# GpSimd sums half of the shift pieces of three quarters, and five small moves around them

## What is computed

```python
c_act = jax.nn.silu(c)
mod = c_act @ w_ada[l] + b_ada[l]                 # 2048 x 6144, one row
shift, scale, gate = jnp.split(mod, 3, axis=-1)
h = rms_norm(x, norm_g[l]) * (1 + scale[:, None]) + shift[:, None]
proj = h @ w_in[l]                                # 256 x 2048 times 2048 x 13824
pool_u, pool_z, q, k, v, attn_z, conv_a, conv_b, conv_z, gates = jnp.split(proj, split_idx, axis=-1)
# three branches (trailing-window pooling, windowed attention, gated causal convolution),
# each times silu of its z, projected, times its sigmoid gate, summed to merged
x = x + gate[:, None] * (merged @ w_out[l])
return rms_norm(x, final_g)
```

## Time and profile before

| | us |
|---|---|
| median of 3 runs | 956.42 (956.16 to 956.43) |
| the profiled execution | 956.62 |
| its span in the trace | 954.8 |
| TensorE busy in the span | 914.2 (96%) |
| VectorE busy | 686.2 (72%) |
| ScalarE busy | 417.4 (44%) |
| GpSimd busy | 10.0 (1%) |

### The profile page before, as it was taken

The page is one execution under the profiler, slowest core; times in us unless marked ns, Lnnn a source line. Parts: engine busy times, 40 slices in busy tenths (PEclk is TensorE's granted clock), DMA queues, the critical chain, the costliest instruction groups (busy, mean ns, idle before and its releaser), DMA issues.

```text
span 954.8 us, 10317 instructions
## 1 busy us (share of the span) xinstructions
PE 914.2 (96%) x4243; PEld 740.6 (78%) x4243; DVE 686.2 (72%) x793; ACT 417.4 (44%) x375; POOL 10.0 (1%) x27
## 2 busy tenths in 40 slices
PE   1799999989999999999999999999999999999996
PEld 1467686878888888888888888888888888887884
DVE  4767696768968867767778776595677878756663
ACT  3436152634344343443474655447433333434332
POOL 2000000000000000000000000000000000000000
PEclk9899999999999999999999999999999999999998
DMA  9999999855446565665544444554779998955512
GB/s 327 382 387 387 360 366 352 301 161 172 140 154 220 178 206 189 189 208 176 177 158 155 140 166 137 174 178 171 243 247 393 375 329 304 323 188 198 176 45 88
DMA packets 107790, 220.01 MB, mean 230 GB/s; under 512 B 3696, under 2 KB 3776, under 8 KB 106976
## 3 DMA queue, kind: packets, MB, share of 16 engines
q1 hardware_dynamic: 106336, 212.88, 64.7%
q0 software_dynamic: 1120, 5.43, 1.5%
q10 hardware_dynamic: 288, 1.05, 0.3%
HBM read 217.25 MB, written 2.10 MB: 230 GB/s over the span
## 4 chain that ended last, share of the span: by engine, by line
PE 88%; DMA 5%; DVE 3%; ACT 2%; issue 1%; SPq 0%; DVEq 0%; ACTq 0%
PE acc_odd L1107 13%; PE acc_odd L1109 13%; PE acc_even L1107 13%; PE acc_odd L1108 13%; PE acc_even L1109 12%; PE acc_even L1108 12%; DMA raw<-in_w_in 4%; PE side_a L1107 1%; ACT wh L429 1%; PE side_a L1109 1%; PE side_a L1108 1%; DVE wl L679 1%; DMA x_tok<-in_x 1%; PE side_b L1278 1%; DVE ada_sums L716 1%
## 5 line engine op out<-in xcount | busy, mean ns | idle before, releaser
L679 DVE TENSOR_TENSOR wl<-raw,wh 128x2048 fp32r<-128x2048 f32 x151 | 345.4, 2290 | 195.5 <-ACT wh L429 195.0
L429 ACT ACTIVATE wh<-raw 128x2048 fp32r<-128x2048 f32 x151 | 288.3, 1913 | 290.1 <-PE acc_even L1109 114.5
L1107 PE MATMUL acc_even<-wh,act_h 128*128 128x512 f32 x432 | 172.5, 399 | 6.0 <-DVE wl L727 3.2
L1107 PE MATMUL acc_odd<-wh,act_h 128*128 128x512 f32 x432 | 170.0, 394 | 0.7 <-DVE part_u L772 0.7
L1109 PE MATMUL acc_even<-wh,act_l 128*128 128x512 f32 x432 | 169.3, 392 | 0.0
L1108 PE MATMUL acc_even<-wl,act_h 128*128 128x512 f32 x432 | 169.2, 392 | 0.0
L1109 PE MATMUL acc_odd<-wh,act_l 128*128 128x512 f32 x432 | 168.3, 390 | 0.0
L1108 PE MATMUL acc_odd<-wl,act_h 128*128 128x512 f32 x432 | 168.1, 389 | 0.0
L1107 PEld LDWEIGHTS acc_even<-wh,act_h 128*128 128x128 f32 x432 | 81.8, 189 | 25.6 <-issue 4.6
L847 DVE SCALAR_TENSOR_TENSOR conv_slots<-conv_slots,taps 128x256 f32<-128x256 f32 x240 | 100.2, 479 | 0.2
L1107 PEld LDWEIGHTS acc_odd<-wh,act_h 128*128 128x128 f32 x432 | 81.1, 188 | 18.3 <-DVE part_u L772 1.1
(11 more groups left out here) (270 smaller groups left out, 892.6 us busy)
## 6 DMA issues: line engine op xcount, KB each, us to landing
raw<-in_w_in SPq DMA_DIRECT2D x107, 1024.0 KB, 5.1
raw<-in_w_ada SPq DMA_DIRECT2D x48, 1024.0 KB, 9.1
raw<-in_w_out SPq DMA_DIRECT2D x16, 1024.0 KB, 5.0
raw<-in_w_branch_pool SPq DMA_DIRECT2D x8, 1024.0 KB, 5.0
raw<-in_w_branch_attn SPq DMA_DIRECT2D x8, 1024.0 KB, 5.0
raw<-in_w_branch_conv SPq DMA_DIRECT2D x8, 1024.0 KB, 6.0
raw<-in_conv_pw SPq DMA_DIRECT2D x4, 1024.0 KB, 5.1
x_tok<-in_x SPq DMA_DIRECT2D x2, 1024.0 KB, 8.9
```

What stands on the lines that cost most here:

```text
L429: nc.scalar.activation(wh[:, m % RING], raw[SLOT_OF[g]][:, :, :], ACT.Copy).then_inc(high_done, 1)
L679: nc.vector.tensor_tensor(wl[:, m % RING], raw[SLOT_OF[load_of(m)]][:, :, :], wh[:, m % RING].bitcast(F32), ALU.subtract).then_inc(raw_don ...
L1107: nc.tensor.matmul(sums, xh, wh[:, slot, i, :], start=begin, stop=False)
```

## The change

Six edits. First, of the four shift pieces of each of the quarters 1 to 3, pieces 0 and 1 are no longer multiplied by TensorE: GpSimd multiplies each of their row tiles with its column of c (in place), and adds them up in `gate_sums`, a buffer that is unused at that time: 7 instructions for piece 0 and 8 for piece 1, each waiting for the one before. The slot is free when GpSimd is done. TensorE reduces that sum over partitions with four one-column matmuls behind the scale sums, and VectorE adds the four columns to the shift. Pieces 2 and 3 stay at j = 3 and 4. Second, `pool_w` is loaded behind all this and behind the last `h_ready`. Third, the low half of the very first piece is made tile by tile, so that TensorE may start on tile 0. Fourth, from `glu_a` on, VectorE takes each last part one step earlier. Fifth, so it does with the low halves of `merged` near the end (steps 131 to 137 in place of 132 to 138). Sixth, the last scaling is shared 1280 : 768 columns between VectorE and ScalarE in place of 1024 : 1024, and the stores with it.

```diff
+def by_pool(load):
+    return load[0] == "shift" and load[1] > 0 and load[2] < 2
...
-    HALF = D_MODEL // 2
+    SHARE = 1280
...
-                if before >= 0 and LOADS[before][0] == "shift":
-                    sp.wait_ge(shift_done, shifts(before))
+                if before >= 0 and by_pool(LOADS[before]):
+                    sp.wait_ge(pool_summed, pool_shifts(before))
+                elif before >= 0 and LOADS[before][0] == "shift":
+                    sp.wait_ge(shift_done, pe_shifts(before))
...
-            pool.wait_ge(x_t, 4)
+            pool.wait_ge(consts_ready, 1)
+            pool.wait_ge(c_ready, 1)
+            for q in range(1, QUARTERS):
+                if q > 1:
+                    pool.wait_ge(mod_t, q)
+                for i in range(2):
+                    g = LOAD_OF["shift", q, i]
+                    pool.wait_ge(loaded[SLOT_OF[g]], landed(g))
+                    for t in range(PK):
+                        src, column = raw[SLOT_OF[g]][:, t, :], c_act[:, PK * i + t:PK * i + t + 1]
+                        dst = src if i or t else gate_sums[:, :]
+                        last = nc.gpsimd.tensor_tensor(dst, src, column.broadcast_to([P, COLS]), ALU.mult)
+                        if i or t:
+                            chained(last)
+                            last = nc.gpsimd.tensor_tensor(gate_sums[:, :], gate_sums[:, :], src, ALU.add)
+                        if t < PK - 1:
+                            chained(last)
+                    last.then_inc(pool_summed, 1)
+                    pool.wait_ge(pool_summed, 2 * q - 1 + i)
+            pool.wait_ge(h_ready, KT)
             pool.dma_start(pool_w[:, :, :, :], a["pool_w"][0].rearrange("g (k p) n -> p g k n", p=P)
                            ).then_inc(pool_w_loaded, 16)
-            pool.wait_ge(h_ready, KT)
...
+            def first_split_tile(t):
+                dve.wait_ge(first_high, 1)
+                nc.vector.tensor_tensor(wl[:, 0, t, :], raw[SLOT_OF[load_of(0)]][:, t, :], wh[:, 0, t, :].bitcast(F32),
+                                        ALU.subtract).then_inc(first_low, 1)
...
+                if q:
+                    chained(nc.vector.tensor_tensor(mod_shift, mod_shift, pb[:, 1 + PK:1 + 2 * PK], ALU.add))
...
             hidden_tile(0)
-            first_split(0)
+            first_split_tile(0)
             hidden_tile(1)
-            first_split(1)
+            first_split_tile(1)
+            first_split_rest()
...
-                if m == 23:
+                if m == 22:
                     dve.wait_ge(*freed("b0"))
...
-                if m in (24, 25, 26, 27, 28):
-                    last_part(OPEN[m - 22])
+                if m in (23, 24, 25, 26, 27):
+                    last_part(OPEN[m - 21])
...
-                if m in (132, 134, 136, 138):
-                    j = (m - 132) // 2
+                if m in (131, 133, 135, 137):
+                    j = (m - 131) // 2
...
-                half = x_res[:, h, 0:HALF]
+                half = x_res[:, h, 0:SHARE]
...
-                if q and i == 0:
+                first = 2 if q else 0
+                if q and i == first:
                     pe.wait_ge(mod_ready, q)
...
                 if q:
-                    ins = scale_sums(q)
+                    scale_sums(q)
+                    pe.wait_ge(pool_summed, pool_shifts(LOAD_OF["shift", q, 3]))
+                    for t in range(PK):
+                        ins = nc.tensor.matmul(pb[:, 1 + PK + t:2 + PK + t], gate_sums[:, P * t:P * (t + 1)], ones[:, 0:1],
+                                               start=True, stop=True)
...
-                    if 1 <= j < 5:
+                    if 3 <= j < 5:
                         shift_piece(k + 1, j - 1)
```

More of the change, by code:

```diff
@@ L95, in shifts, with pool_shifts, pe_shifts @@
     return sum(load[0] == "shift" for load in LOADS[:g + 1])
+def by_pool(load):
+    return load[0] == "shift" and load[1] > 0 and load[2] < 2
+def pool_shifts(g):
+    return sum(by_pool(load) for load in LOADS[:g + 1])
+def pe_shifts(g):
+    return shifts(g) - pool_shifts(g)
 def raws(g):
@@ L454, in copy_shift @@
             def copy_shift(q):
-                spread(shift_rows[:, :], pb[:, 0:COLS], shift_done, 4 * (q + 1), shift_copied)
+                spread(shift_rows[:, :], pb[:, 0:COLS], shift_done, pe_shifts(LOAD_OF["shift", q, 3]), shift_copied)
             def first_split(half):
@@ L661, in _ @@
                 act.wait_ge(rstd_ready, h + 1)
-                half = x_res[:, h, HALF:D_MODEL]
+                half = x_res[:, h, SHARE:D_MODEL]
                 nc.scalar.activation(half, half, ACT.Copy, scale=out_rstd[:, h:h + 1]).then_inc(out_high, 1)
                 act.wait_ge(out_high, h + 1)
-                act.dma_start(out_rows[:, h, HALF:D_MODEL], half).then_inc(stored, 16)
+                act.dma_start(out_rows[:, h, SHARE:D_MODEL], half).then_inc(stored, 16)
         @block.vector
@@ L720, in scale_piece, with first_split_rest @@
                 last.then_inc(raw_done, 1)
-            def first_split(half):
-                g = load_of(0)
-                tiles = slice(PK // 2 * half, PK // 2 * (half + 1))
-                dve.wait_ge(high_done if half else first_high, 1)
-                nc.vector.tensor_tensor(wl[:, 0, tiles, :], raw[SLOT_OF[g]][:, tiles, :],
-                                        wh[:, 0, tiles, :].bitcast(F32), ALU.subtract
-                                        ).then_inc(raw_done if half else first_low, 1)
+            def first_split_rest():
+                tiles = slice(PK // 2, PK)
+                dve.wait_ge(high_done, 1)
+                nc.vector.tensor_tensor(wl[:, 0, tiles, :], raw[SLOT_OF[load_of(0)]][:, tiles, :],
+                                        wh[:, 0, tiles, :].bitcast(F32), ALU.subtract).then_inc(raw_done, 1)
+            def first_split_tile(t):
+                dve.wait_ge(first_high, 1)
+                nc.vector.tensor_tensor(wl[:, 0, t, :], raw[SLOT_OF[load_of(0)]][:, t, :], wh[:, 0, t, :].bitcast(F32),
+                                        ALU.subtract).then_inc(first_low, 1)
             def modulation_columns(q):
@@ L1149, in shift_piece @@
                     ins = nc.tensor.matmul(pb[rows, 0:COLS], c_wide[:, PK * i + t, :], raw[SLOT_OF[g]][:, t, :],
-                                           start=(i == 0), stop=(i == 3), tile_position=(0, QUAD * t))
+                                           start=(i == first), stop=(i == 3), tile_position=(0, QUAD * t))
                 ins.then_inc(shift_done, 1)
```

8 lines of the change are left out of this document (4 added, 4 removed).

## The result

| | us |
|---|---|
| before, median of 4 runs beside it | 956.42 (956.16 to 956.83) |
| changed kernel, median of 4 runs | 973.61 (973.21 to 973.99) |
| ratio, 95% interval | 1.018 (1.016 to 1.020) |
| profiled execution after, and its span | 973.62, 971.8 |

The change makes the kernel 17.2 us slower. The forecast was 947.6, the range ended at 970. It is rival C's outcome, in its time and in its cause.

The account below looks back on a forecast made before the run. TensorE, busy 88% of the span, was taken as the bound, with loads deciding in quarter 0. Terms -1.85 - 2 x 1.47 - 3.9 - 0.1 = -8.8 gave 947.6 us as median; range 945.5 to 970.

Parts of the forecast that it names:

- rival C: VectorE and GpSimd exclude each other when reading SBUF; slots and later quarters late: 968 to 976 us, chance 0.28.
- GpSimd's price: One 512-column GpSimd instruction on shift pieces: 1.24 us plus 0.1 for the semaphore, 1.35; upper bound 3.5.
- the hole: Gap in the load stream when piece 1's slot is freed late: 0.9 us in quarter 0, covered in quarters 1 and 2.
- case A: The forecast itself, GpSimd at 1.35 us: 947.6 us, 946.8 if no hole opens, 950.5 at 1.45 us; chance 0.48.
- The break-even of 1.61 us: Average GpSimd instruction time, waits included, at which the whole change's sum is zero; above it the kernel is slower.
- some 3 us sooner: How much earlier the slots would be free by the skill's GpSimd figure, 1.12 us for 512 columns.
- TensorE's share: Per quarter: two fewer shift pieces -2.38, four new matmuls +0.81, a stall +0.1: -1.47 us.
- The slope of 15 T: With T us per GpSimd instruction, the quarter 0 hole is 15 T - 19.35; it counts later when above 2.35.
- The limit of 64.1: Latest time in us to issue the load reusing piece 1's slot in quarter 0 without a hole; forecast issue 65.0.
- Quarter 0: Piece 6 waits for loads; the pooling weights' departure brings it 2.71 us earlier, less the hole: -1.85 us.
- Last parts and low halves: Later steps: four TensorE waits for VectorE vanish with the order turned, restarts included: -3.9 us.
- The tail: Last scaling shared 1280 : 768 between VectorE and ScalarE: between -0.29 and +0.19, taken as -0.1 us.

Follow-up runs that it names:

- writes_long: The changed kernel with each GpSimd instruction replaced by three or four memsets that read nothing, 1.94 us an instruction; shift lacks pieces 0 and 1: 975.65 us.
- ghost_reads: The changed kernel without its first edit, plus GpSimd's 45 instructions on its own buffer, holding no slot, sums unused: 954.81 us.
- the memset kernels: The changed kernel with GpSimd's instructions replaced by memset chains: writes_short 946.74 us, writes_only 966.65 us, writes_long 975.65 us.
- writes_short: The changed kernel with each GpSimd instruction replaced by two memsets that read nothing, 1.17 us an instruction; shift lacks pieces 0 and 1: 946.74 us.
- writes_only: The changed kernel with each GpSimd instruction replaced by three memsets that read nothing, 1.75 us an instruction; shift lacks pieces 0 and 1: 966.65 us.
- moves_only: The changed kernel with the first edit undone (all shift pieces back on TensorE), the other five kept: 950.84 us.
- pool_w_only: The kernel before, with only the load of `pool_w` moved behind the last `h_ready`: 955.60 us.

## Why the prediction was wrong

**The step that failed is GpSimd's price**, 1.35 us, "since ... I see nothing in the trace in which the two engines held each other up". A trace in which GpSimd reads nothing while VectorE works can't show that, and rival C's own text said so. The memsets of the earlier trace rows were the wrong neighbour for a second reason: a memset doesn't wait for VectorE, 0.53 us in writes_long beside a working VectorE. The instruction's own time was even over-priced (1.24, measured 1.04); the turns added 0.82 to each 1.12. Put into the prediction's own sum, the measured pace gives 15 x 1.94 - 19.35 = 9.75 for the hole and 9.75 - 3.82 = 5.93 for each later quarter: -2.71 + 9.75 + 2 x 5.93 - 4.0 = +14.9, 971.5 us against the measured 973.6. That it comes so near is in part luck, since the later quarters lost their time at VectorE and the clock and not at the load that this sum speaks of. One time given for case A was wrong as a sum: at 1.45 us an instruction it comes to 956.6 - 7.2 = 949.4, not 950.5.

**Rival C had the cause and the outcome.** It let piece 0 end at 61.7 and piece 1 at 77; they ended at 58.94 and 73.11. It gave +10.3 for piece 6, measured +7.45, and "2.6 each at the least, some 7 with holes of their own" for a later quarter, measured +7.57 and +6.51: the upper end. Its 968 to 976 holds 973.6. Both of its ways are in the trace, the slot that comes late in quarter 0, and behind it a VectorE without a pause that TensorE waits for. Its sum of both engines' times fits less well: with the measured 1.04 it is 28.5 + 15.6 = 44.1 us, less than the 44.47 of a quarter, and ghost_reads, where the two take turns and nothing is held, has 46.01 and 45.17, not the 47.1. And no case had the time at the lower clock, 3.6 us in each later quarter. The break-even of 1.61 us lies between the points on record, 1.17 and 1.75; back from 966.65 at 45 us for each us of pace, an estimate from the memset kernels, it would be 1.52.
The Trainium skill, SBUF — State Buffer, section Who interferes with whom, calls this an exclusive lock; the trace agrees, instruction by instruction, with 2.97 us for a GpSimd instruction behind a split against 1.04 alone.
The Trainium skill, GPSIMD Engine Reference, section Performance versus the Vector engine, has 4497 ns for 2048 columns; a quarter of it, an estimate, is 1.12 us for one instruction; measured is 1.04. The prediction's "some 3 us sooner" compares it with 1.35; with the 0.1 between two instructions kept, fifteen times 0.12 is 1.8.

**The rest of case A held.** TensorE's share was forecast at -1.47 a quarter; writes_short has 43.04 for 44.47 and 43.03 for 44.37, -1.4. The slope of 15 T for the hole holds: from writes_only to writes_long the late issue moves from 70.33 to 73.49 and piece 6 from 86.46 to 89.48. The limit of 64.1 was some 1 us too kind: piece 6 begins 16.0 to 16.1 us behind the late issue in both and in the changed kernel, and 78.95 - 16.05 = 62.9. The later quarters lose more than the sum has, but not by the load: writes_only loses 49.54 - 43.04 = 6.5 in quarter 1, where 15 x 1.75 - 19.35 - 2.35 gives 4.6. TensorE's one wait there, for a load at 124.51, is 3.87 us. The other 2.6 come behind it, where the granted clock is 0.50 from 124 to 130 us; the sum had no such term.

**Quarter 0** was put at -1.85 with the hole and -2.75 without. writes_short, without a hole, shows -2.79, but not as the text had it: moves_only, with the same late `pool_w` and all shift pieces on TensorE, shows only -1.36. So about half came from TensorE's share, which was to buy nothing there, and about half from the other moves; the departure of `pool_w` alone was worth 0.9, not 2.7.

**Last parts and low halves**: -3.9 forecast for four waits. All four are gone in the changed kernel. From piece 21 to VectorE's last scaling it is 949.70 - 176.12 = 773.58 us before and 966.53 - 197.66 = 768.87 after: -4.7. Nine other kernels with these moves have 768.75 to 769.01, and pool_w_only, without them, 773.38. So the term was 0.8 too small.

**The tail**: -0.1 forecast. From the start of the last scaling to the span's end it is 5.13 us before and in pool_w_only, and 5.26 to 5.28 in every kernel with the new shares: +0.14. In the last scaling, VectorE then ScalarE:

```profile
966.53 0.88 DVE L1139 TENSOR_SCALAR x_res<-x_res,small 128x1280 f32<-128x1280 f32 x1
...
966.58 0.93 ACT L697 ACTIVATE x_res<-x_res,small 128x768 f32<-128x768 f32 x1 [1.23 <-DVEq L1137]
```

The two engines now end 0.1 us apart, where it was 0.45, and the end still comes 0.14 later: the shares of 1280 and 768 columns cost a little in place of the 0.1 that they were to give. Why is not shown.

**What the chances should have been**: what decided was one unmeasured property, with an argument for C and none against it that the trace could bear. C would move the time by 20 us and more and no row spoke against it, so it deserved more than 0.28; and a range that ends at 970 took in only the lowest quarter of C's 968 to 976.

## What to carry to other kernels

Work given to GpSimd isn't free because GpSimd is idle: ask first whether VectorE's instructions there read SBUF, with two operands above all, and price each engine by what it takes beside the other (here 1.94 us for 1.12, and 1.5 for 0.78), not alone. Then ask two things: who waits for the slower instruction to give a buffer back, and who waits for the slowed VectorE itself. Here each way alone could cost most of the loss, so relieving one of them gave back less than half; look at the other before you add the gain up.

The best complete kernel of this study leaves the sums on TensorE and keeps the five small moves: 950.84 us, 0.6% faster than before.

## What the runs showed of the hardware

- GpSimd and VectorE take turns, instruction by instruction, even on unrelated data (ghost_reads): four scale sums go from 3.11 us to 5.87 (6.37 in the changed kernel), a split from 2.29 to 3.12, a tap of 256 columns from 0.42 to 1.2, GpSimd's 128x512 product from 1.04 to 2.97.
- The turns overlap a little: in the changed kernel GpSimd starts an instruction each 1.57 us beside scale sums (59.02 to 62.16, two of them), where the two alone add up to 1.04 + 0.78 = 1.82.
- One-input products of VectorE from SBUF to SBUF (301.29 and 306.83 above) are held up too, 0.37 to 1.1 us each. VectorE's product with one input from PSUM (327.86) isn't: 1.21 us beside GpSimd, 1.22 in moves_only.
- A GpSimd memset, which only writes, neither waits nor makes VectorE wait: 0.53 us for 512 columns beside splits of 2.29.
- A wait of TensorE can cost more than its length: behind one of 3.87 us (writes_only) the granted clock was 0.50 from 124 to 130 us, which cost 2.6 more; behind one of 0.62 us (moves_only) it stayed at 1.00.
